# Down weights of experts 16 to 29 as one 4 MB load each, and SwiGLU rows turned by sixteen 64x64 products instead of four 128x128

## What is computed

```python
N_EXPERTS = 32; TOP_K = 4; D_MODEL = D_FF = 1024
def expert_block(xblk, e):                 # the tokens that chose expert e
    gu = xblk @ w_gu[e] + b_gu[e]          # w_gu[e] is 1024 x 2048, 8 MB
    gate, up = jnp.split(gu, 2, axis=-1)
    gate = jnp.minimum(gate, 7.0)
    up = jnp.clip(up, -7.0, 7.0)
    hid = (up + 1.0) * (gate * jax.nn.sigmoid(gate * 1.702))
    return hid @ w_dn[e] + b_dn[e]         # w_dn[e] is 1024 x 1024, 4 MB
# the rows are weighted by the gates and added to their tokens
```

## Time and profile before

| | us |
|---|---|
| Median of 3 runs | 1174.85 (1174.79 to 1176.46) |
| The profiled execution, its own time | 1177.47 |
| Its span in the profile | 1175.5 |
| TensorE busy | 1113.1 (95%) |
| TensorE weight loads busy | 546.3 (46%) |
| VectorE busy | 309.2 (26%) |
| ScalarE busy | 185.6 (16%) |
| DMA | 437.92 MB, mean 373 GB/s |
| Chain that ended last | PE 57%, DMA 40% |

### The profile page before, as it was taken

The page is one execution under the profiler, slowest core; times in us unless marked ns, Lnnn a source line. Parts: engine busy times, 40 slices in busy tenths (PEclk is TensorE's granted clock), DMA queues, the critical chain, the costliest instruction groups (busy, mean ns, idle before and its releaser), DMA issues.

```text
span 1175.5 us, 12276 instructions
## 1 busy us (share of the span) xinstructions
PE 1113.1 (95%) x5262; PEld 546.3 (46%) x5263; DVE 309.2 (26%) x599; ACT 185.6 (16%) x329; POOL 20.3 (2%) x46
## 2 busy tenths in 40 slices
PE   9999999999999999999998889999989999989997
PEld 7777676444444443333333334443434343433356
DVE  3156742312221231112111211121112111211135
ACT  3151151111111111111110111111111111101133
POOL 4001000000000000000000000000000000000000
PEclk9999999999999999999999999999999999999999
DMA  9463589999999999999999999999999999999941
GB/s 240 125 172 86 150 278 429 383 418 414 428 420 430 428 427 427 427 428 428 427 428 432 430 429 432 429 433 428 429 428 429 431 428 430 431 430 425 423 169 42
DMA packets 78000, 437.92 MB, mean 373 GB/s; under 512 B 6316, under 2 KB 54712, under 8 KB 56952
## 3 DMA queue, kind: packets, MB, share of 16 engines
q1 hardware_dynamic: 74224, 434.01, 90.1%
q10 hardware_dynamic: 3304, 2.55, 0.7%
q0 software_dynamic: 416, 0.54, 0.2%
HBM read 432.35 MB, written 4.72 MB: 372 GB/s over the span
## 4 chain that ended last, share of the span: by engine, by line
PE 57%; DMA 40%; DVE 1%; ACT 1%; issue 0%; ACTq 0%; POOL 0%; DVEq 0%; POOLq 0%
PE ps L1060 55%; DMA ring<-in_w_gu 28%; DMA ring<-in_w_dn 7%; DMA late_pair<-in_w_dn 2%; DMA ring<-in_w_ple_gate 2%; PE ps L1523 1%; DVE ring L1878 0%; DVE acc L1757 0%; PE ps L1081 0%; PE ps L1560 0%; PE ps L1358 0%; PE ps L1685 0%; DVE tok L1760 0%; PE ps L1174 0%; ACT tok L793 0%
## 5 line engine op out<-in xcount | busy, mean ns | idle before, releaser
L1060 PE MATMUL ps<-ring,aT 128*64 128x512 f32 x976 | 216.9, 598 | 13.3 <-DMA ring<-in_w_gu 11.9
L1060 PE MATMUL ps<-ring,s 128*64 128x512 f32 x912 | 207.0, 607 | 15.5 <-DMA ring<-in_w_gu 15.5
L1060 PE MATMUL ps<-ring,wst 128*64 128x512 f32 x768 | 172.6, 595 | 15.4 <-DMA ring<-in_w_dn 15.3
L2067 DVE TENSOR_SCALAR wst<-ps 128x512 f32<-128x512 f32 x32 | 22.1, 692 | 459.4 <-PE ps L1060 459.4
L1060 PEld LDWEIGHTS ps<-ring,aT 128*64 128x64 f32 x976 | 69.3, 137 | 148.7 <-issue 128.0
L1060 PEld LDWEIGHTS ps<-ring,s 128*64 128x64 f32 x912 | 64.2, 139 | 146.7 <-issue 121.1
L1060 PEld LDWEIGHTS ps<-ring,wst 128*64 128x64 f32 x768 | 55.1, 137 | 125.1 <-issue 112.2
L1060 PE MATMUL ps<-aT,wst 128*128 128x288 f32 x384 | 97.6, 410 | 0.0
L957 ACT ACTIVATE wst<-wst 128x512 f32<-128x512 f32 x32 | 20.2, 630 | 472.5 <-DVE wst L2067 472.5
L1060 PE MATMUL ps<-sel,tok 128*128 128x256 f32 (+1 forms) x432 | 93.4, 358 | 0.0
L1060 PEld LDWEIGHTS ps<-aT,wst 128*128 128x128 f32 x384 | 71.6, 190 | 21.6 <-issue 1.2
(11 more groups left out here) (273 smaller groups left out, 705.5 us busy)
## 6 DMA issues: line engine op xcount, KB each, us to landing
ring<-in_w_gu SPq DMA_DIRECT2D x30, 4096.0 KB, 21.9
ring<-in_w_gu SPq DMA_DIRECT2D x58, 2048.0 KB, 22.7
ring<-in_w_dn SPq DMA_DIRECT2D x47, 2048.0 KB, 26.7
late_pair<-in_w_dn SPq DMA_DIRECT2D x15, 2048.0 KB, 26.9
late_pair<-in_w_gu SPq DMA_DIRECT2D x9, 2048.0 KB, 18.0
wst<-in_w_in SPq DMA_DIRECT2D x28, 512.0 KB, 4.0
ring<-in_w_ple_gate SPq DMA_DIRECT2D x4, 1024.0 KB, 26.5
ring<-in_state_hgrn SPq DMA_DIRECT2D x4, 512.0 KB, 6.0
```

The costliest lines, as they stand in the source:

```text
L1060: return pe.matmul(o, lhsT, rhs, start=start, stop=stop, skip_group_check=True)
L2067: dve.tensor_scalar(gbuf, ps[:, gu_bank(e, 0), :], SWIGLU_LIMIT, None, ALU.min).then_inc(gate_ready, 1)
```

## The change

Down weights: `wide_dn` reads the 1024 rows of `w_dn[e]` with eight neighbouring rows (32 KB) for each partition. For experts 16 to 29 that is one load of 4 MB into a pair of places. For the other experts the two halves of these runs are two loads of 2 MB, of 16 KB out of every 32 KB. With it the plan of places changes: the rule for `free` pairs goes, every pair goes to the one whose last use lies furthest back, and `late_pair` is left empty from the last down unit of expert 15 to the first unit of expert 31.

The turn: because partition p now holds rows 8p to 8p+7, the hidden rows have to be turned so that every eighth column comes together, over 64 partitions at a time: sixteen ordinary products with a 64x64 part of the identity, in place of four transposes. The branch for extra blocks gets the same, and a `keep_busy` product ahead of it.

```diff
+        def wide_dn(e):
+            return io["w_dn"][0, e].rearrange("(p k) n -> p (k n)", k=DN_UNITS * ROWS_DN)
+
         def unit_src(e, c):
 
             if c < GU_UNITS:
                 return wide_src(e, c // 2)[:, c % 2 * UCOLS:(c % 2 + 1) * UCOLS]
-            c, n = c - GU_UNITS, ROWS_DN * P
-            return io["w_dn"][0, e, c * n:(c + 1) * n, :].rearrange("(p k) n -> p (k n)", k=ROWS_DN)
+            return wide_dn(e)[:, (c - GU_UNITS) * UCOLS:(c - GU_UNITS + 1) * UCOLS]
...
-            return e in WIDE and c < GU_UNITS
+            return e in WIDE and (c < GU_UNITS or e < WIDE[-1])
...
             if wide(u) and c % 2 == 0:
-                if c == 0:
-                    free = list(pairs)
-                pair = min(free, key=lambda p: max(held[p[0]], held[p[1]]))
-                free.remove(pair)
+                pair = min(pairs, key=lambda p: max(held[p[0]], held[p[1]]))
             if wide(u):
                 i = pair[c % 2]
-            elif e + 1 in WIDE and c >= GU_UNITS:
-                i = next(k for k, _ in queue if k in free[0] or k == V_SLOT)
             else:
                 i = queue[0][0]
...
-                    sp.dma_start(ring[:, i * UCOLS:(i + 2) * UCOLS], wide_src(e, c // 2)).then_inc(place_loaded[sem_of[u]], 16)
+                    src = wide_src(e, c // 2) if c < GU_UNITS else wide_dn(e)
+                    sp.dma_start(ring[:, i * UCOLS:(i + 2) * UCOLS], src).then_inc(place_loaded[sem_of[u]], 16)
...
             def hid_cols(k):
 
-                return ubuf.rearrange("p (f k) -> p k f", k=ROWS_DN)[:, k, :]
+                return ubuf.rearrange("p (f k) -> p k f", k=DN_UNITS * ROWS_DN)[:, k, :]
+
+            def turn_rows(bank):
+
+                for k in range(DN_UNITS * ROWS_DN):
+                    for r in (slice(0, SLOTS), slice(SLOTS, P)):
+                        ins = mm(ps[r, bank, k * SLOTS:(k + 1) * SLOTS], hid_cols(k)[r], ident[r, r], True, True)
+                return ins
 
             def turn_hidden(e):
 
                 pe.wait_ge(hid_ready, e + 1)
                 if e >= 2:
                     pe.wait_ge(st_copied, e // 2)
-                for k in range(ROWS_DN):
-                    ins = pe.transpose(ps[:, 3, k * P:(k + 1) * P], hid_cols(k), ident[:])
-                ins.then_inc(hT_done, 1)
+                turn_rows(3).then_inc(hT_done, 1)
...
-                        x0 = k * P + c * SLOTS
+                        x0 = (c * ROWS_DN + k) * SLOTS
```

More of the change, by code:

```diff
@@ L1634, in extra_block @@
                 pe.wait_ge(ov_hid, n + 1)
-                for k in range(ROWS_DN):
-                    ins = pe.transpose(ps[:, 4, k * P:(k + 1) * P], hid_cols(k), ident[:])
-                ins.then_inc(ov_hT_done, 1)
+                keep_busy(4, 1)
+                turn_rows(4).then_inc(ov_hT_done, 1)
                 pe.wait_ge(ov_hT_copied, n + 1)
```

## The result

| | us |
|---|---|
| Before, median of 5 runs beside the changed kernel | 1175.26 (1174.79 to 1176.46) |
| The changed kernel, median of 5 | 1186.00 (1185.14 to 1189.34) |
| Ratio | 1.0092, 95% interval 1.0081 to 1.0104 |
| The profiled execution, its own time | 1185.14 |
| Its span | 1183.2 |

The forecast was 1175.8 with a range up to 1180.0; the change costs 10.7 us and lies outside it.

What follows compares the result with a forecast made beforehand. The prediction took the stream of weights to bound the kernel; rate -1.4, front +1.1 and end +1.2 gave +0.9 us on a median of 1174.85, so 1175.8 us, range 1172.3 to 1180.0.

Steps and rivals of the forecast that it cites:

- +0.7 us a turn: Each expert's turn: 32 records take 1.34 us where it took 0.68, so +0.7 us (bounds 0 and +2.8).
- Rival (b): The turn's records go one after another: 3.5 us a turn, +9.4, 1184 us; decides from about 1.9 us; chance 0.07.
- later turns should add nothing: Front: only the turns of experts 0 and 1 delay the gated load, +1.1 us (bounds 0 and +5.3); later ones nothing.
- The merge in the stream: Down loads of experts 16 to 29: each merge saves 0.10 us, 14 together -1.4 us (bounds -1.0 and -2.1).
- The queue in the wide stage: Wide stage: the load of 1014.38 keeps 7.4 us of its 11.0 us lead; the queue doesn't run dry, cost nothing.
- rival (d): Every load has a fixed cost, 2.4 us, that merging removes: 14 merges save 34 us, 1141 us; chance 0.02.
- The end: After the last loads: expert 29's second down half 2.9 us late, plus turns, less waits, leaves +1.2 us (bounds 0 and +5.5).
- Rival (a): The clock drops ahead of the last down products after a merged wait of about 2.4 us: +2.6, 1177.5 us; chance 0.20.

Runs made afterwards that it cites:

- e8: The kernel before with merged down loads in two 16 KB runs, old four transposes, and pads in the turns of experts 30 and 31: 1179.69 us, 1.0033.

## Why the prediction was wrong

**The turn: the term that was mis-sized.** The step "I take 1.34, the row with the same array parts: +0.7 us a turn" failed. The turn takes 2.07 us, so the extra is 1.4 us by rows and 1.5 from start to start. That row had the same array parts but a contiguous stationary side; it was nearest in shape and not in what sets the pace. The prediction named the stride ("read at every eighth element") and gave it nothing, because four strided 128x128 loads fitted in 0.68 us. Sorted columns brought the turn to 1.08 us, so without the stride the estimate would even have been high, and the stride costs about 1.0 us. Rival (b) had said that from 1.9 us on the sum passes 0.2%; that point was right (the turn took 2.07 and the sum passed it), and the chance of 0.07 given to it only covered its own extreme of 3.5 us. What lay between 1.34 and 3.5 had no case. The runs agree in direction with a rule that the prediction should have weighed (the Trainium skill, Advanced Engine Details and Errata, section Memory Cachelines: reads of SBUF are slower where each falls into another 16-byte line). They don't agree with it in size. Every fourth and every eighth float32 are both in lines of their own; yet sorting them took a tenth off the pace in the first case (120 to 109 ns for a transpose) and half in the second (120 to 58 ns for a pair of loads). The page gives no amount. Whether a 128x128 load at every eighth element would also take twice as long, no run shows.

**The front: "later turns should add nothing" failed.** With 1.4 us, two turns give 2 x 1.4 - 0.29 = +2.5, and the pad in two turns measured that (1.0021). But the changed kernel's landings are 2.1 us later at the load of 282.29, 3.4 after the load of 292.67, 4.1 at 320 us, 6.0 at 370 us and 4.5 from 440 to 500 us. The rule can be read from rows: a 2 MB load issued into an empty queue lands 7.2 to 7.3 us after its issue, and in the full stream 4.9 after its forerunner, so it is gated (it lands late for having been issued late) once its lead, the time from its issue to its forerunner's landing, falls below 7.3 - 4.9 = 2.4 us. Each load then allows a delay of the tensor engine of (lead - 2.4), and the delay grows with each turn ahead of it. The load of 288.35: three turns, 4.3 - (3.31 - 2.4) = 3.4. The load of 327.45, whose lead was 3.82 (forerunner at 331.27): four turns, and in the changed kernel it was issued at 333.35, so 5.9 - 1.4 = 4.5. The load of 372.90, lead 8.71: nothing more. The largest counts, 4.5 us.

That the landings behind 440 us are also 4.5 us late is in part luck. Just ahead of 400 us the execution of before had one step that was 1.5 us too long, which took that much off the distance: 6.0 at 370 us, 4.5 behind it. The landing of the same load in three traces, the changed kernel, the kernel before, and the kernel before with pads at the end alone:

```profile
437.45 0.33 SPq L646 DMA_DIRECT2D ring<-in_w_gu  x1
425.21 0.33 SPq L648 DMA_DIRECT2D ring<-in_w_gu  x1
424.56 0.33 SPq L648 DMA_DIRECT2D ring<-in_w_gu  x1
```
```profile
ring<-in_w_gu SPq DMA_DIRECT2D x1, 2048.0 KB, 13.8
ring<-in_w_gu SPq DMA_DIRECT2D x1, 2048.0 KB, 21.5
ring<-in_w_gu SPq DMA_DIRECT2D x1, 2048.0 KB, 20.2
```

That is 451.2, 446.7 and 444.8 us. The five kernels whose front is that of before (pads in the middle or at the end, merge alone, and the two with sorted transposes) have 444.8 to 445.5; the turn alone and the changed kernel with the last load split have 451.9 and 452.2. So the front costs about 6 us, of which the rule explains 4.5; the rest isn't explained. The prediction looked at the load that was already gated and not at those which 1.4 us a turn would bring there; at its own 0.7 us a turn this rule gives 4 x 0.7 - 1.4 = 1.4, so the omission cost little there and much at the true size.

**The merge in the stream: the step was right, the saving didn't come.** A merged load landed 9.71 us after its forerunner. The 9.83 of the prediction came from landings rounded to 0.1 us; read to 0.01 us, two down loads take 9.78. That saves 0.07 us a merge, 14 x 0.07 = 1.0 us, the prediction's lower bound. Between the landings of experts 16 and 30 the time is nevertheless 411.6 against 410.6 us: single steps that are 0.2 to 2.9 us too long occur in every trace of this study at changing places. In this stretch the changed kernel's execution had five of them, 3.8 us over the regular step together, and that of before one of 1.6 us. The seven traced kernels with merged loads had 2.0 to 5.9 us of them (mean 3.9), the eight without 1.5 to 3.1 (mean 2.3). One execution of each is no proof, but it points to a price of the merge in the stream that the prediction put at nothing, of the size of what it saves. What makes these steps long wasn't found.

**The queue in the wide stage: right, with less room.** The load that was to keep 7.4 us keeps 6.40; the smallest lead for a first gate/up load was 3.3 us, at 792 us, behind two experts with more products. From turn to turn these kept the engine busy for 31.0 and 31.4 us, more than the 29.26 of the stream (29.5 and 29.9 in the kernel before), and the lead took that up. It didn't run dry, and fourteen pads for experts 8 to 21 in the kernel before cost nothing. (For the fixed part of a load that rival (d) names, the prediction cites 2.0 us; the cited section gives it for loads issued by GpSimd, and those here are SyncE's, with 2.3 to 2.4.)

**The end: the grain was right, the sum too small.** Second half at landing + 4.7, 2.9 us late: e8's rows have 1089.62 - 1084.87 = 4.75, and with pads at the end 2.8 us were measured for 2.7. Put in 1.4 for 0.7 and the prediction's own sum is 2.9 + 1.4 - 0.6 + 1.4 - 2.4 = +2.7, not +1.2.

**Rival (a) came true on top.** The page of the changed kernel has TensorE busy in 98% of the span and still the clock fell: the unit of 1089.15 took 5.35 us, not 3.65, with a granted clock of 0.59 from 1089 to 1092 us, mostly the 1.2 GHz level: +1.7. With the load split it took 3.60 and the clock wasn't low. The argument against it, that 2.4 us of waiting is less than the 2.65 that had brought the clock down before, failed: it fell after 2.25. These are single executions. In the merge with pads at the end the clock didn't fall at this place, after a wait of 1.93, so that it was the split that kept it up in the other kernel is likely and not shown. From the late load to the row of 1101.24 the terms are 5.1 + 2.9 + 1.7 + 1.4 - 0.6 = 10.5, and the rows have 10.46. The four waits give back 2.4, the turn of expert 31 adds 1.4, which makes 9.4; the row after the last `w_ple_gate` wait is 8.8 us later than before. The other 0.6 came back because a wait that is gone takes more with it than its own idle time: from the row of 1095.14 to that of 1110.00, with its wait of 0.91, are 14.86 us before, and 13.79 (1104.01 to 1117.80) in the turn alone, which has the old places and no wait there.

**The sum again**, between the two profiled executions: front 451.2 - 446.7 = +4.5, from there to the last landing of expert weights 677.0 against 677.9 us, -0.9, and from that landing to the end 54.93 against 50.87 us, +4.1 (the terms for the end had given 2.7 + 1.7 = 4.4). Together that is the 7.7 us between the spans. The medians differ by 10.7. Two things close most of the gap: the front, which against the five other kernels costs 5.7 to 6.4 us and not 4.5, and the 0.9 us by which the profiled execution of the changed kernel stood below its median. Less than 1 us stays open. It isn't particular to the change, since the merge with pads has the same ratio.

## What to carry to other kernels

When an operand is read at another stride, don't price the operation by a row with the same shape: look which side sets the pace, and take the row with the same access, or bound it from above: here every eighth element cost twice the contiguous load, every fourth a tenth more. Work that is hidden in the middle of a stream isn't hidden where its queue is short: for each load take its lead over the landing before it, less the lead at which a load is gated, and set against that the delay of all turns ahead of that load, not only of those ahead of the first gated one. Two edits that are each absorbed at the end can use the same slack; add their delays before subtracting the waits.

## What the runs showed of the hardware

- 64x64 float32 stationary loads, alternating between two parts of the array, started in pairs 5 to 7 ns apart; the pairs went every 120 ns read at every eighth element and every 58 ns contiguous (64.0 and 32.3 us over 1024 records). For 128x128 transposes read at every fourth element the difference was smaller: one every 120 ns against 109 (17.8 against 13.4 us of load time over 128 records).
- A 4 MB load with 32 KB runs landed 9.71 us after its forerunner, one with two runs of 16 KB for each partition 9.78, as two loads of 2 MB did (medians of 14 in the changed kernel and in the merge alone).
- VectorE's product of 128x512 took 1064 ns when read and written at a stride, against 692 ns.
- The length of a single wait doesn't decide on the clock: after 2.52 us (the unit at 1060.01) the unit took its usual 3.65 us, after 2.25 us (1089.15) it took 5.35.
